# A hybrid decoder step with 16,384 single-neuron experts: u and v tiles loaded in pairs of halves, SyncE's program written out

## The reference, cut to what matters

```python
u_rows = p['peer_u'][idx]                      # idx: 8 heads x 16 experts for each token
act = jax.nn.gelu(jnp.einsum('phkd,pd->phk', u_rows, xb).astype(jnp.float32))
coef = (gates * act).astype(xb.dtype)
return jnp.einsum('phk,phkd->pd', coef, p['peer_v'][idx])
```

## Time and profile before

| | |
|---|---|
| median of three runs | 4364.22 us (4346.82, 4364.22, 4369.38) |
| span of the profiled execution | 4329.5 us |
| PE busy in the span | 3728.3 us (86%) |
| DVE busy | 3020.4 us (70%) |
| POOL busy | 2050.1 us (47%) |
| ACT busy | 1466.9 us (34%) |
| moved | 1090.68 MB, mean 252 GB/s |
| mean granted TensorE clock | 0.942 |
| 2300 to 4180 us: DMA share, rate | 1.00 and 0.99; 396 and 398 GB/s |

### The profile page before, as it was taken

The page is one execution under the profiler, slowest core; times in us unless marked ns, Lnnn a source line. Parts: engine busy times, 40 slices in busy tenths (PEclk is TensorE's granted clock), DMA queues, the critical chain, the costliest instruction groups (busy, mean ns, idle before and its releaser), DMA issues. The chain is left out here.

```text
span 4329.5 us, 66268 instructions
## 1 busy us (share of the span) xinstructions
PE 3728.3 (86%) x24298; PEld 3467.2 (80%) x24298; DVE 3020.4 (70%) x4791; ACT 1466.9 (34%) x1882; POOL 2050.1 (47%) x1144
## 2 busy tenths in 40 slices
PE   6786998999897898997678989899998888889986
PEld 3336888988886797997568888888988888888986
DVE  5777645455545224798977777777778788888886
ACT  5665343434443113222332332332332322232232
POOL 2343222222223233334046776677676667677672
PEclk9997999999998898998999999999999999999998
DMA  8981222222223122222489999999999999999994
GB/s 310 346 335 52 83 81 83 74 71 70 64 79 103 52 99 102 82 74 92 169 326 382 401 405 384 378 405 407 398 397 376 389 393 405 399 405 414 410 407 172
DMA packets 253137, 1090.68 MB, mean 252 GB/s; under 512 B 25353, under 2 KB 78857, under 8 KB 172297
## 3 DMA queue, kind: packets, MB, share of 16 engines
q1 hardware_dynamic: 167440, 543.60, 34.1%
q0 software_dynamic: 73728, 536.90, 30.4%
q10 hardware_dynamic: 11776, 7.52, 0.6%
HBM read 1047.54 MB, written 40.40 MB: 251 GB/s over the span
## 5 line engine op out<-in xcount | busy, mean ns | idle before, releaser
L248 POOL TENSOR_TENSOR wlo<-raw,whi 128x1024 fp32r<-128x1024 f32 x551 | 1342.6, 2440 | 1436.7 <-ACT whi L244 1431.0
L244 ACT CAST whi<-raw 128x1024 fp32r<-128x1024 f32 x670 | 697.2, 1049 | 1241.4 <-DMA raw<-in_u 554.8
L263 PE MATMUL gps<-hi_d,whi 128*128 128x320 f32 x2048 | 661.1, 323 | 126.4 <-POOL wlo L248 69.4
L2095 PE MATMUL gps<-chi,whi 128*128 128x320 f32 x2048 | 655.7, 320 | 111.6 <-DVE outacc L2224 83.8
L263 PE MATMUL gps<-lo_d,whi 128*128 128x320 f32 x2048 | 651.2, 318 | 0.0
L263 PE MATMUL gps<-hi_d,wlo 128*128 128x320 f32 x2048 | 650.4, 318 | 0.0
L2095 PE MATMUL gps<-clo,whi 128*128 128x320 f32 x2048 | 644.4, 315 | 0.0
L2095 PE MATMUL gps<-chi,wlo 128*128 128x320 f32 x2048 | 644.3, 315 | 0.0
L2182 DVE SCALAR_TENSOR_TENSOR dps<-ring,coef,dps 128x2048 f32<-128x2048 f32 x252 | 591.9, 2349 | 4.3 <-DVE dps L2182 0.5
L2169 DVE CUSTOM_DVE_ANT_0 ring<-ring,dps 128x2048 f32<-128x2048 f32 x256 | 582.3, 2279 | 0.0
L263 PEld LDWEIGHTS gps<-hi_d,whi 128*128 128x128 f32 x2048 | 401.6, 196 | 146.7 <-POOL wlo L248 78.6
(11 more groups left out here) (384 smaller groups left out, 5947.0 us busy)
## 6 DMA issues: line engine op xcount, KB each, us to landing
raw<-in_u SPq DMA_DIRECT2D x256, 512.0 KB, 9.5
raw<-in_v SPq DMA_DIRECT2D x256, 512.0 KB, 7.9
wada<-in_w_ada SPq DMA_DIRECT2D x96, 1024.0 KB, 6.3
raw<-in_w_in SPq DMA_DIRECT2D x96, 512.0 KB, 3.5
gateD<-gst SPq DMA_DIRECT2D x8, 2560.0 KB, 7.6
gate<-gateD SPq DMA_DIRECT2D x32, 640.0 KB, 17.1
raw<-in_w_out SPq DMA_DIRECT2D x32, 512.0 KB, 3.8
raw<-in_w_q SPq DMA_DIRECT2D x32, 512.0 KB, 4.0
```

What stands on the lines that cost most here:

```text
L244: act.copy(whi[:, k.slot, :], raw_of(k)).then_inc(W.hi, 1)
L248: pool.tensor_tensor(wlo[:, k.slot, :], raw_of(k), whi[:, k.slot, :].bitcast(F32), ALU.subtract).then_inc(W.lo, 1)
L263: m = pe.matmul(gps[:, bank, 0:DT], w, x[:, kt, :], start=(kt == 0 and n == 0), stop=(kt == KT - 1 and n == 2))
L2095: m = pe.matmul(gps[:, 2 + dt, 0:DT], w[:, slot, cols], x[:, buf, c, :], start=(c == 0 and n == 0), stop=(c == NG - 1 and n == 2))
```

## The change

Halves become pairs. `u` is laid out in HBM by whole tiles (128 partitions x 8192 bytes) and `v` by pairs of halves of the same size. `load_pair` loads both raw buffers of `raw` or of `raw2` with one transfer of 1 MB, after it has waited for the low parts of both halves that stood there. Both halves are then covered by the one semaphore of the pair's first buffer. The order of the halves, the buffers, the splits and the matmuls are unchanged. The first 16 halves of `u`, in the stage before, are still loaded one by one, out of the new layout. SyncE's program for the expert stage is written out by `unrolled_groups` instead of run in loops, and the conditions that told loop turns from single ones are replaced by comparisons of the group number.

```diff
+        def load_pair(sp, t, n, k):
+
+            back = 4 if k.c >= N_DEEP + 2 else 2
+            sp.wait_ge(*lo_done(k.plus(-back)))
+            sp.wait_ge(*lo_done(k.plus(1 - back)))
+            pair = pairs[raw_at(k) // 2]
+            sp.dma_start(pair[:, :, :].rearrange("p a f -> p (a f)"), row(t, n)).then_inc(w_loaded[raw_at(k)], 16)
+
         def split_hi(act, k):
-            act.wait_ge(w_loaded[raw_at(k)], loads(k))
+            act.wait_ge(w_loaded[raw_at(k) // 2 * 2 if deep(k) else raw_at(k)], loads(k))
...
                     for n in range(8 * EARLY):
-                        load_half(sp, a["u"][n], Nth(N7 + n))
-                    for n in range(2):
-                        load_half(sp, a["v"][n], Nth(N7 + 8 * EARLY + n))
+                        load_half(sp, a["u"][n // 2][:, n % 2 * HALF:(n % 2 + 1) * HALF], Nth(N7 + n))
+                    load_pair(sp, a["v"], 0, Nth(N7 + 8 * EARLY))
...
                     def load_gates(g, buf):
-                        if not isinstance(g, int):
+                        if g >= EARLY:
                             sp.wait_ge(S.gated, g * NG - NG)
...
                     def A(g, buf, k, after):
-                        for j in range(2 * NG):
-                            if j == 0:
-                                load_gates(g, buf)
-                            if j < 6:
-                                load_half(sp, row(a["u"], g * 8 + (j + 2)), k.plus(j + 2))
-                            else:
-                                load_half(sp, row(a["v"], g * 8 + (j - 6 - 8)), after.plus(j - 6))
+                        load_gates(g, buf)
+                        for j in range(1, NG):
+                            load_pair(sp, a["u"], g * 4 + j, k.plus(2 * j))
+                        load_pair(sp, a["v"], g * 4 - 4, after)
 
                     def B(g, buf, k, after):
                         for s in range(8):
-                            if s < 6:
-                                load_half(sp, row(a["v"], g * 8 + (s + 2)), k.plus(s + 2))
-                            elif not isinstance(g, int):
-                                load_half(sp, row(a["u"], g * 8 + (s - 6 + 16)), after.plus(s - 6))
-                            elif after is not None:
-                                load_half(sp, row(a["v"], g * 8 + (s - 6 + 8)), after.plus(s - 6))
-                            if isinstance(g, int) and after is not None and s >= 4:
+                            if s % 2 == 0 and s < 6:
+                                load_pair(sp, a["v"], g * 4 + (s // 2 + 1), k.plus(s + 2))
+                            elif s == 6 and g < NGRP - 2:
+                                load_pair(sp, a["u"], g * 4 + 8, after)
+                            elif s == 6 and after is not None:
+                                load_pair(sp, a["v"], g * 4 + 4, after)
+                            if g == NGRP - 2 and s >= 4:
                                 sp.wait_ge(W.used, N7 + 16 * NGRP - 16)
...
-                    groups(sp, A, B)
+                    unrolled_groups(A, B)
...
-    u = np_("peer_u")[0].reshape(NKEY, P, 2, 8, P).transpose(0, 2, 4, 3, 1)
-    v = np_("peer_v")[0].reshape(NGRP, NG, P, 8, 2 * P).transpose(0, 3, 2, 1, 4)
+    u = np_("peer_u")[0].reshape(NKEY, P, 2, 8, P).transpose(0, 4, 2, 3, 1)
+    v = np_("peer_v")[0].reshape(NGRP, NG, P, 4, 2, 2 * P).transpose(0, 3, 2, 4, 1, 5)
```

More of the change, by code:

```diff
@@ L197, in build @@
         raws = [raw[:, 0, :], raw[:, 1, :]]
+        pairs = [raw]
         N_SHARED = 2 + 12 * H + 2 * KT + 4 * H + 18
@@ L1916, in build @@
         raws += [raw2[:, 0, :], raw2[:, 1, :]]
+        pairs += [raw2]
         rings += [sb(f"ring{n}", [P, D], at=at7) for n in range(RING0, RING)]
@@ L2355, in layout @@
         "keys": np.ascontiguousarray(np_("peer_subkeys")[0].transpose(0, 1, 3, 2)).reshape(2 * H, P, NKEY),
-        "u": np.ascontiguousarray(u).reshape(2 * NKEY, P, HALF),
-        "v": np.ascontiguousarray(v).reshape(8 * NGRP, P, HALF),
+        "u": np.ascontiguousarray(u).reshape(NKEY, P, 2 * HALF),
+        "v": np.ascontiguousarray(v).reshape(4 * NGRP, P, 2 * HALF),
         "u_rows": np_("peer_u")[0],
```

## The result

The change makes the kernel slower: 4487.59 us (median of 4 runs, 4477.13 to 4497.26) against 4366.80 us (4 runs, 4346.82 to 4383.52). The ratio is 1.0282, with a 95% interval of 1.0245 to 1.0319. I had forecast 4349 us and a range up to 4400. The profiled execution has a span of 4487.3 us. That is 2 us under its run's time, as in every other run here, while the span of 4329.5 us that stands for the kernel before is 37 us under the median: that execution was a short one. The 34.7 us that the prediction added to a span was no fixed offset, and comparisons of these two traces make the loss some 35 us too large. A fairer partner, w_out_halves, follows among the experiments.

What follows compares the result with a forecast made beforehand. DMA bytes, not TensorE, were taken to bound the expert stage. Terms of -20 + 5 = -15 us, the others 0, took the 4329.5 us span to 4314.5; adding 34.7 us gave 4349 us, range 4290 to 4400.

Steps and rivals of the forecast that it cites:

- Step 2: In `load_pair`, waiting for both low parts issues the first half later, but existing waiting time covers it: 0.
- the rival of the cycle: At `load_pair`'s wait for the second low part, the pair's cycle sets the pace: +96 us, 4460; chance 0.13.
- Step 1: In the `u` and `v` loads, packets of 8192 instead of 4096 bytes take less engine time per byte: -20 us.
- The dear-packets rival: In SyncE's queue, 1 MB loads in 8 KB pieces cost more per byte: +26 + 5, 4395 at worst; chance 0.12.
- Step 3: SyncE's queue is empty more often between a landed pair and the next issue: +5 us, ends 0 and +16.
- Steps 4, 5 and 6: Gate load behind the first pair; SyncE's written-out program; first `x2T` reload in `B(30)` behind a pair: 0 each.
- Step 6: In `B(30)`, the first `x2T` reload is issued up to 4 us later behind a pair, which is covered: 0.
- The rival of more turns: Among the DMA queues, larger packets get SyncE's queue more of the turns: 45 us more gained, 4299; chance 0.20.

Runs made afterwards that it cites:

- w_out_halves: The changed kernel with its written-out program and new layout, but every half loaded by itself in 4096-byte pieces: 4358.08 us, 1.0010 of the kernel before.
- coarse_v_only: w_out_halves with pairs of `v` alone issued after both low parts and used only when both halves have landed: 4499.15 us, 1.0354 of the kernel before.
- joint_arrival: w_out_halves, but rounding of a pair's first half waits until both halves have landed: 4451.06 us, 1.0228 of the kernel before.
- coarse_u_only: w_out_halves with pairs of `u` alone issued after both low parts and used only when both halves have landed: 4388.91 us, 1.0076 of the kernel before.
- one_transfer_4k: The changed kernel with the old layout, so one 1 MB transfer per pair goes in 4096-byte pieces: 4515.18 us, 1.0375 of the kernel before.
- wide_gates_halves: w_out_halves with gates laid out in HBM by partition and group, loaded in 5120-byte pieces: 4287.58 us, 0.9849 of the kernel before.
- wide_early_halves: wide_gates_halves with VectorE's low parts in the `u` phase moved ahead of its wait for gelu: 4256.41 us, 0.9769 of the kernel before.
- early_low_halves: w_out_halves with VectorE's low parts in the `u` phase moved ahead of its wait for gelu: 4341.76 us, 0.9975 of the kernel before.

## Why the prediction was wrong

**Step 2 failed, and with it the sum.** I took 0 for the wait for both low parts, because 3.2 us of lateness stood against 4.8 us that a half waits anyway, both as averages over the stage. Late issue costs 74 us, joint arrival 99 us, and they add where VectorE's low parts come late. Three things were wrong in it.

- The lateness was an average over issues that are not alike. Neighbours were taken as 4.0 us apart; but every fourth low part is VectorE's, at the end of a long line in `A`. In the turns shown, (v0, v1) is issued 9.6 us later behind its gate load than v0 was (40.6 less 31.0), of which 6.5 us is that low part (40.6 against 34.1 with it early); averaged over all turns, 11.4 us (41.4 less 29.9) and 6.2.
- The 4.8 us of cover was an average too. The `v` phase had too little of it, which coarse_v_only shows: a new wait of 115.8 us.
- Joint arrival had no price of its own; it stood only in the landing time of the pair. joint_arrival leaves every issue rule as it was and costs 99 us. How much of this is again the second half held up by VectorE was not tried: no run has joint arrival alone with early low parts.

**Its landing was mis-sized.** 7.0 us worked out; 8.7 and 10.2 measured. The prediction could have seen this: by the same working a single half lands in 1.85 + 3.9 = 5.8 us, where the trace had 7.8 and 9.6, and it then set the worked-out pair against the measured half. The cycle with the measured values is 10.2 + 7.3 = 17.5 us for `u` and 16.0 for `v`, against a turn of 16.7 before and 72.16 / 4 = 18.0 after. It took GpSimd for both low parts, while in every other pair the second is VectorE's. So the rival of the cycle, at 0.13, had the place right (the wait for the second low part) and the direction. That its price was near (96 us, 121 measured) is partly luck, for it put all on the pairs of `u`, and in coarse_u_only and coarse_v_only `v` bears more than four fifths; with the measured landing of `v` it would have given nothing for `v`.

**Step 1 had the right sign, and its size holds only beside the same transfer in smaller pieces.** Against one_transfer_4k the rates give 21 us and the kernels differ by 41; with early low parts the pieces are worth 0.4% at most. Against the kernel before, SyncE's queue fell only from 41.8 to 41.3 engine-us per MB, and that of the rows rose from 39.3 to 0.610 x 30080 / 454.29 = 40.4, so that no engine time was saved in a turn (67.3 us, 66.6 before). The dear-packets rival is out, for it wanted over 42 in SyncE's queue.

**Step 3, and the reading behind it.** I allowed 5 us for an emptier queue. The share of 0.93 and 0.94 in place of 1.00 is the loss itself, seen from the DMA side. "Bytes set the pace" was too strong a reading of a share of 1.00: later issues cost 74 us all the same, and the new layout of the gates gained 66 at 407 GB/s and more. Its own test, a share well below 0.98 with PE no busier, is what came.

**Steps 4, 5 and 6 held nearly**, as far as the runs show: coarse_u_only costs 33 us for all pairs of `u`, little but not nothing, and w_out_halves none. Step 6 was not tried by itself; the turns account for nearly the whole difference. The rival of more turns asked for rows that land in over 10 us and PE waits under 80; the rows land in 8.5 and 9.8 us, the waits went to 226, so it is out for this kernel.

**Open** remains why two transfers with a late issue profit so little from the early low parts (16 us), what the last 35 to 39 us between pairs and halves are, late issue or joint arrival, and why larger pieces gain twice what the rates give.

## What to carry to other kernels

When two buffers become one, look up who releases each, and where in that engine's program the release stands: the pair inherits the latest of the two, in every turn, and an average over the stage hides it. Merging transfers buys a little by its larger pieces (here 41 us beside the same transfer in small ones) and pays with both a later issue and a later first use, two costs that added here (74 + 99 us). Check also whether the execution that was profiled is a typical one, before its span is set against a median. A load in small pieces at the head of a queue can be worth several times its bytes: re-laying 20 MB of gates gained 66 us, priced at 14.

## What the runs showed of the hardware

In SyncE's queue pieces of 8192 bytes beside 4096, in the same transfer of 1 MB, lowered the engine time of a byte by 3% (42.6 to 41.3 engine-us per MB), the landing of `v` by 0.9 us and that of `u` by 0.1, and the kernel's time by 0.9%. The Trainium skill (DMA: Bandwidth & Descriptors, Specifications) gives line rate from 512 bytes; the runs here still show a gain between 4096 and 8192. Unexpected was the gate load: with 5120-byte pieces it still lands in 12.6 us in wide_gates_halves and 13.6 in wide_early_halves, with 8 packets an engine in place of 64 (it is issued right behind two halves of `u`), yet wide_early_halves is 2% faster than early_low_halves. The prediction took the 17.1 us as a sign that turns go by packets; an eighth of the packets did not bring the landing under 12.6, so their number is a part of it at most.
